# Routing the prompt rows of layer one during sample attention, with the eight sample rows as extra columns of the first two expert tiles

## The reference, cut to what matters

```python
xp = layer_norm(ALPHA * xp + mix_p, ln1_g[i], ln1_b[i])
xs = layer_norm(ALPHA * xs + mix_s, ln1_g[i], ln1_b[i])
xp = layer_norm(ALPHA * xp + moe(xp, ...), ln2_g[i], ln2_b[i])
xs = layer_norm(ALPHA * xs + moe(xs, ...), ln2_g[i], ln2_b[i])

def moe(x, w_router, router_bias, w_gate, w_up, w_down):
    combine = route(t, w_router, router_bias)          # two nonzero weights a row
    h = silu(einsum('td,edf->tef', t, w_gate)) * einsum('td,edf->tef', t, w_up)
    y = einsum('tef,efd->td', h * combine[:, :, None], w_down)
```

## Time and profile before

| what | value |
|---|---|
| median of 3 runs | 1125.22 us (1124.78 to 1127.2) |
| the profiled execution, its own time | 1126.03 us |
| its span, first to last instruction | 1124.4 us |
| mean granted TensorE clock | 0.938 of full |
| PE busy | 978.1 us, 87% of the span |
| DVE busy | 376.1 us, 33% |
| ACT busy | 195.2 us, 17% |
| POOL busy | 94.5 us, 8% |
| HBM traffic | 255.88 MB read, 40.11 MB written |

### The profile page before, as it was taken

One profiled execution on the slowest core, in us unless ns is written; L12 is line 12 of the kernel. 1 busy time (PEld: TensorE's weight loads), 2 busy tenths in 40 slices (PEclk: granted clock), 3 DMA queues, 4 the chain that ended last, 5 costly groups with the idle time before them and its releaser, 6 DMA issues.

```text
span 1124.4 us, 36091 instructions
## 1 busy us (share of the span) xinstructions
PE 978.1 (87%) x15881; PEld 836.7 (74%) x15881; DVE 376.1 (33%) x825; ACT 195.2 (17%) x441; POOL 94.5 (8%) x179
## 2 busy tenths in 40 slices
PE   7979999989998329999999997783399999999975
PEld 6857777754566128999999996562389999999962
DVE  1234443423364612122122122796112122122127
ACT  1233434430052020000000001111200000001010
POOL 0002112141010030000000001200200000000011
PEclk8989999999999559999999999895699999999998
DMA  9513244614311979999999995790599999999935
GB/s 336 189 54 91 89 135 127 206 43 137 92 48 64 412 272 332 361 405 380 403 388 397 381 389 189 269 354 9 194 368 366 407 388 391 393 380 384 396 118 201
DMA packets 80249, 296.26 MB, mean 263 GB/s; under 512 B 10200, under 2 KB 40288, under 8 KB 71871
## 3 DMA queue, kind: packets, MB, share of 16 engines
q1 hardware_dynamic: 52343, 246.53, 58.5%
q10 hardware_dynamic: 19712, 26.75, 7.1%
q0 software_dynamic: 8144, 22.29, 5.7%
HBM read 255.88 MB, written 40.11 MB: 263 GB/s over the span
## 4 chain that ended last, share of the span: by engine, by line
PE 79%; DVE 10%; DMA 4%; issue 3%; POOL 2%; ACT 1%; ACTq 0%; SPq 0%; POOLq 0%; DVEq 0%
PE PS L924 16%; PE PS L945 15%; PE PS L934 15%; PE PS L840 5%; PE PS L598 4%; PE PS L910 3%; PE PS L645 3%; PE PS L661 2%; PE PS L554 2%; PE PS L654 2%; PE PS L576 2%; POOL expert_rows L1106 2%; PE PS L749 1%; PE PS L618 1%; PE PS L635 1%
## 5 line engine op out<-in xcount | busy, mean ns | idle before, releaser
L924 PE MATMUL PS<-arena,ring 128*64 128x96 f32 x4096 | 185.4, 249 | 52.6 <-DVE arena L1759 52.4
L924 PEld LDWEIGHTS PS<-arena,ring 128*64 128x64 f32 x4096 | 175.1, 139 | 59.3 <-issue 59.3
L945 PE MATMUL PS<-arena,ring 128*64 128x96 f32 x4096 | 175.4, 246 | 2.5 <-issue 2.0
L934 PE MATMUL PS<-arena,ring 128*64 128x96 f32 x4096 | 175.0, 246 | 2.8 <-issue 2.8
L945 PEld LDWEIGHTS PS<-arena,ring 128*64 128x64 f32 x4096 | 171.3, 137 | 3.2 <-issue 2.5
L934 PEld LDWEIGHTS PS<-arena,ring 128*64 128x64 f32 x4096 | 171.2, 137 | 3.1 <-issue 3.1
L1759 DVE STREAM_TRANSPOSE arena<-arena 128x768 uint32<-128x768 uint32 x34 | 54.2, 1595 | 166.7 <-ACT arena L1311 138.4
L1784 DVE COPY arena<-PS 128x384 f32<-128x384 f32 x32 | 17.9, 558 | 164.3 <-PE PS L945 164.3
L1313 ACT ACTIVATE arena<-PS 128x384 f32<-128x384 f32 x32 | 15.7, 490 | 265.5 <-PE PS L945 265.5
L840 PE MATMUL PS<-ring,arena 128*128 128x512 f32 x128 | 55.6, 593 | 0.7 <-issue 0.7
L598 PE MATMUL PS<-arena,ring 128*128 128x260 f32 x192 | 46.8, 395 | 2.3 <-POOL ring L1057 2.0
(11 more groups left out here) (276 smaller groups left out, 1030.1 us busy)
## 6 DMA issues: line engine op xcount, KB each, us to landing
ring<-w_gate SPq DMA_DIRECT2D x32, 2048.0 KB, 14.8
ring<-w_up SPq DMA_DIRECT2D x32, 2048.0 KB, 16.1
ring<-w_down SPq DMA_DIRECT2D x32, 2048.0 KB, 17.9
arena<-expert_rows ACTq DMA_DIRECT2D x144, 96.0 KB, 9.0
expert_out<-arena ACTq DMA_DIRECT2D x32, 384.0 KB, 11.8
expert_rows<-ring SPq DMA_DIRECT2D x6, 1920.0 KB, 10.2
ring<-cache_ckv SPq DMA_DIRECT2D x56, 128.0 KB, 2.2
ring<-w_o SPq DMA_DIRECT2D x1, 4096.0 KB, 19.3
```

The costliest lines, as they stand in the source:

```text
L924: last = nc.tensor.matmul(bank(s, KF, CAP)[at:at + 64, f, :], wg[w][:, k, P * f + at:P * f + at + 64], xeT[s][:, k, :], start=(k == 0), st ...
L934: last = nc.tensor.matmul(out[at:at + 64, :], wu[w][:, k, P * f + at:P * f + at + 64], xeT[s][:, k, :], start=(k == 0), stop=(k == KD - 1))
L945: last = nc.tensor.matmul(bank(4 + m // 4, 4, CAP)[at:at + 64, m % 4, :], wd[w][:, f, P * m + at:P * m + at + 64], h[s][:, f, :], start=(f ...
```

## The change

In layer one only, routing is split in two (`choose`, `assign`), each over a range of row tiles:

- The four prompt tiles are routed inside `samples`: `router(0, 3)` moves from u = 3 to u = 1, `choose` over tiles 0 to 3 follows DVE's step u = 1, `counts` moves into PE's step u = 2, and `assign` with the table of tiles follows DVE's step u = 2. POOL scatters the eight prompt row groups as soon as their indices are there.
- The table is made before the sample rows are routed. So `reserve` adds 8 rows to the demand of each expert but the first two, and the sample rows find room if they choose it. `NOV`, the most overflow tiles, goes from 10 to 12.
- The first two experts (tiles 0 and 1) take all eight sample rows as extra columns, 104 instead of 96 (`WIDE`). Their rows come from on-chip transposes of the normalised rows (`turn_sample_rows`), and the results go through `turn_sample_out` and a store of 16 rows of their own.
- The sample rows themselves are routed (`router(0, 4)`, `choose(0, 2, 4, 5)`, `counts(2, ...)`, `assign(0, 2, 4, 5)`) while tiles 0 and 1 run, and scattered to the other experts; a constant `dense_row` points to the 16 rows where they chose expert 0 or 1. Rows of tiles 2 and 3 are loaded after that scatter.
- SP issues the first weights one by one (up and down of expert 0 earlier than before, gate of expert 0 when the pages are done, gate and up of expert 1 after the output projection) and also loads the prompt rows of the first two tiles.
- ACT scales the four prompt row tiles behind sample attention, ahead of the square root of `norm(0, 0, 4)`.
- PE's code has tiles 0 and 1 written out ahead of the loop, which starts at the second pair.
- Scratch regions move in the arena, and `latent_q` uses whole 128-row matmuls in place of halves. Functions without a caller are deleted.

```diff
             def samples():
                 for u in range(BATCHES):
...
-                    if u == BATCHES - 1:
+                    if u == 1:
+                        pe.wait_ge(tp_ev[0], 15)
+                        pe.wait_ge(tp_ev[1], 15)
                         router(0, 3)
+                    elif u == 2:
+                        counts(1, 0, NT - 1)
...
             pe.wait_ge(uv_ev, 1)
             mix(0, 4)
+            turn_sample_rows()
             router(0, 4)
-            counts(0)
             experts(0)
```

```diff
-                with pe.Fori(0, nh) as u:
+                if L == 0:
+                    pe.sem_inc(q["back_ps"], 1)
+                    pe.wait_ge(dense, 2)
+                    tile(0, 0, WIDE)
+                    tile(0, 1, WIDE)
+                    turn_sample_out()
+                with pe.Fori(1 if L == 0 else 0, nh) as u:
...
+            def turn_sample_out():
+
+                pe.wait_ge(S[0]["yT_set"], 2 * DENSE + 2)
+                for m in range(KD):
+                    last = nc.tensor.transpose(bank(1 + 2 * (m // 4), 4, P)[0:DENSE * DB, m % 4, :], yT_s[:, m, :], ident)
+                last.then_inc(dense, 1)
```

DVE:

```diff
                     if u == 0:
                         norm(0, 0, 3, summed=True)
+                    elif u == 1:
+                        v.memset(r_exp[:, E * (NT - 1):], 1.0).then_inc(lg_zero, 1)
+                        choose(0, 1, 0, NT - 1)
+                    elif u == 2:
+                        assign(0, 1, 0, NT - 1)
...
             norm(0, 0, 4)
-            route(0)
...
+            dve.wait_ge(dense, 1)
+            v.tensor_copy(xeT[WIDE][0][:, :, CAP:], bank(1, KD, DB))
+            v.tensor_copy(xeT[WIDE][1][:, :, CAP:], bank(1, KD, DB)).then_inc(dense, 1)
             experts(0)
```

SP, ACT and POOL:

```diff
-                    load_expert(0, 0, 1, gate_free=(pv_ps, BATCHES + 1))
-                    load_expert(0, 1, 0, gate_free=(mix_ps, NT), down_free=(lg_ps, 1))
+                    sp.wait_ge(pv_ps, 3)
+                    sp.dma_start(wu[1], t["w_up"][0, 0].rearrange("(p k) f -> p k f", p=P)).then_inc(q["wu_ld"][1], 16)
+                    sp.wait_ge(pv_ps, 4)
+                    sp.dma_start(wd[1], t["w_down"][0, 0].rearrange("(k p) d -> p k d", p=P)).then_inc(q["wd_ld"][1], 16)
+                    sp.wait_ge(sc_ps, BATCHES)
+                    sp.dma_start(wd[0], t["w_down"][0, 1].rearrange("(k p) d -> p k d", p=P)).then_inc(q["wd_ld"][0], 16)
+                    sp.wait_ge(pv_ps, 5)
+                    sp.dma_start(wg[1], t["w_gate"][0, 0].rearrange("(p k) f -> p k f", p=P)).then_inc(q["wg_ld"][1], 16)
+                    sp.wait_ge(scat, 128)
+                    load_rows(sp, 0, 0, slice(0, CAP))
+                    load_rows(sp, 0, 1, slice(CAP, 2 * CAP))
+                    sp.wait_ge(mix_ps, NT)
+                    sp.dma_start(wg[0], t["w_gate"][0, 1].rearrange("(p k) f -> p k f", p=P)).then_inc(q["wg_ld"][0], 16)
+                    sp.dma_start(wu[0], t["w_up"][0, 1].rearrange("(p k) f -> p k f", p=P)).then_inc(q["wu_ld"][0], 16)
...
                 take_latent_out(BATCHES - 1)
+                act.wait_ge(scat, 128)
+                for i in range(NT - 1):
+                    scale_rows(i)
...
+            hold(pool_e, idx_set, 2)
+            hold(pool_e, zero_st, 16 * (PAIRS - 1))
+            hold(pool_e, ln_out[0], NT - 1)
+            for i in range(NT - 1):
+                scatter(i)
+
             hold(pool_e, uv_ps, 1)
```

More of the change, by code:

```diff
@@ L35 @@
 KOV = (TOK - 1) // CAP
-NOV = 10
+NOV = 12
+DENSE = 2
+WIDE = CAP + DB
 TILES = E + NOV
@@ L720, in latent_q @@
                     for c in range(MKV):
-                        for at in (0, 64):
-                            last = nc.tensor.matmul(bank(7, MKV, PAIRS, 16)[at:at + 64, c, j, :],
-                                                    wukT[:, j, P * c + at:P * c + at + 64], qs[:, j, :], start=True, stop=True)
+                        last = nc.tensor.matmul(bank(7, MKV, PAIRS, 16)[:, c, j, :], wukT[:, j, P * c:P * (c + 1)], qs[:, j, :],
+                                                start=True, stop=True)
                 last.then_inc(ql_ps, 1)
@@ L923, in tile @@
                             for at in (0, 64):
[L924 to L925 removed]
+                                last = nc.tensor.matmul(bank(s, KF, n)[at:at + 64, f, :], wg[w][:, k, P * f + at:P * f + at + 64],
+                                                        x[:, k, :], start=(k == 0), stop=(k == KD - 1))
                     last.then_inc(q["gate_ps"][s], 1)
                     pe.wait_ge(q["wu_ld"][w], 16 * (u + 1))
+                    if n == WIDE and s == 0:
+                        counts(2, NT - 1, NT)
                     for f in range(KF):
[L931 removed]
+                        out = bank(2 + s, KF, n)[:, f, :] if f < KF - 1 else bank(6 + s, n)
                         for k in range(KD):
@@ L1035, in _ @@
                 router(1, i)
-            counts(1)
+            counts(3, 0, NT)
             experts(1)
@@ new lines, in tile @@
+                    if n == WIDE and s == 0:
+                        assign(0, 2, NT - 1, NT)
+                    elif n == WIDE:
+                        next_rows()
+                    dve.wait_ge(q["down_ps"][s], 2 * u + 2)
+                    if n == WIDE:
+                        v.tensor_copy(yT_s[:, 4:8, DB * s:DB * (s + 1)], bank(5, 4, n)[:, :, CAP:])
+                    v.tensor_copy(yT[:, 4:8, :], bank(5, 4, n)[:, :, 0:CAP]).then_inc(q["yT_set"], 1)
+                tile(0, 0, False, CAP if L else WIDE)
@@ L1793, in _ @@
             dve.wait_ge(act_ev, 4 * PAIRS)
-            v.memset(bank(6, NT * E), 0.0).then_inc(lg_zero, 1)
             for i in range(3):
@@ L1820, in _ @@
                     norm(1, 0, step - 4)
-            route(1)
+            choose(1, 3, 0, NT)
+            assign(1, 3, 0, NT)
             dve.wait_ge(mix_ps, 2 * NT)
```

389 lines of the change are left out of this document (222 added, 167 removed).

## The result

| | before | after |
|---|---|---|
| median of 6 runs each | 1125.07 us (1124.15 to 1127.2) | 1136.34 us (1133.42 to 1140.11) |
| ratio | | 1.0099, 95% interval 1.0077 to 1.012 |
| the profiled execution, its span | 1126.03, 1124.4 us | 1138.04, 1136.3 us |
| PE busy | 978.1 us | 994.4 us |

The change costs 11 us; the forecast was a gain of 9. The prediction had the sign wrong. The median lies outside its range, which ended at 1122.5.

A forecast was written before the change was run, and what follows sets the result against it. PE sets the expert phase's pace, after a 35.5 us gap before it that isn't PE's work. Terms -31.5 + 15.0 + 7.5 = -9.0 us give a median of 1116.2, range 1107.5 to 1122.5.

The forecast's parts named there:

- What leaves the gap: Between normalised sample rows and first expert matmul: of 35.5 us, 4.0 remain, so 31.5 us are removed.
- What the sample phase gains: Prompt routing between the steps of sample attention lengthens that phase by 15.0 us, 11.6 of it by the probabilities of u = 3.
- The clock's 3.4 us: After PE idles some 9 us, last weighing, transposes and sample output projections run at half clock: 3.4 us, ends 0 and 5.
- `latent_q` in whole matmuls, costed at nothing: In latent_q, whole matmuls have the same count of columns per weight load, so the edit costs nothing.
- a fall within six idle microseconds: In sample attention before, PE's clock was at half in the six us for which PE had run dry.
- Eight scatters land by 376.3 if nothing slows them: Prompt row scatters of 0.5 MB take 10.2 us on POOL from 362.8 and land by 376.3, costed at nothing.
- The second rival: Scatter shares DMA engines with weights and lands late, at 389; first matmul 2.5 to 6 us later, 1121 us; chance 0.15.
- Its price at the square root, 3.5 us: If the scatter lands late, ACT's scalings hold back the square root for the sample rows by 3.5 us.
- Loaded by 33 (9.0): Rows of tiles 2 and 3, scattered by 24 us into the expert phase, load in 9.0 us, by 33.
- the third rival: Routing the sample rows isn't hidden: half of tile 2 idles if loads take twice 9 us; gain 5, 1120; chance 0.07.
- New code, 3.5 us: First passages through new code, with tiles 0 and 1 written out, cost 3.5 us more, between 0 and 3.7.
- the first rival: No second price of new code and no early fall of the clock: 16 us gained, 1109; chance 0.17.

The follow-up runs named there:

- Experiments 1 and 6: 1: the changed kernel with latent_q in halves again, 1129.71 us, ratio 1.004; 6: the kernel before with latent_q in whole matmuls, 1128.71 us, ratio 1.002.
- experiment 2: The changed kernel with ACT's four scalings of prompt rows moved behind the exponential of the sample rows' router: 1133.59 us, ratio 1.0064.
- Experiment 3: The changed kernel with the sample rows' counts and slots earlier and the rows of tiles 2 and 3 loaded in tile 0: 1126.18 us, ratio 0.9999.
- experiment 5: The kernel before with only PE's first two tiles of layer one written out ahead of the loop: 1132.95 us, ratio 1.0056.
- experiment 4: The changed kernel with latent_q in halves, ACT's scalings later, and rows of tiles 2 and 3 routed and loaded early, all together: 1117.96 us, ratio 0.9918.

## Why the prediction was wrong

Three steps failed: two landing times and one term put at nothing. Point by point:

- **What leaves the gap** held: from the normalised rows (398.42) to the first expert matmul (402.28) 3.9 us, forecast 4.0.
- **What the sample phase gains** held: the probabilities of u = 3 came at 372.3, forecast 369.7, and those of u = 1 had been 2.35 us late already; `choose` ended at 348.8, `assign` ran from 357.8 to 368.1. The clock's 3.4 us held as a sum (2.9), not in its parts: the last weighing took 1.7 us more and the transposes before it 1.0, but the projections behind it only 0.2, as they had been at half clock before too.
- **`latent_q` in whole matmuls, costed at nothing**, failed. It took 5.48 us instead of 2.02, and the clock was at half from 292 to 298. Busy times by stretch of the kernel after:

```profile
288.00:290.00 2.00, 1.26 (x32) 1.02 (x32) 1.97 (x3) 1.08 (x2) 0.00 (x0) 1.00 0.51 160
290.00:292.00 2.00, 2.00 (x26) 1.97 (x24) 1.86 (x5) 0.29 (x1) 0.00 (x0) 0.98 0.03 8
292.00:294.00 2.00, 2.00 (x11) 2.00 (x11) 1.84 (x2) 0.00 (x0) 0.00 (x0) 0.50 0.21 54
```

  Ahead of the fall PE is busy but for one pause of 0.74 us in front of the router, which stands in every kernel here. So it isn't a fall within six idle microseconds, as I had read the earlier trace rows. That reading was wrong for the kernel before as well: in the first of these rows PE is busy for all of 366 to 368 at 0.50, and the clock had fallen in the two microseconds before, of which PE was busy for 1.45:

```profile
364.00:366.00 2.00, 1.45 (x46) 1.34 (x46) 0.44 (x2) 0.40 (x1) 0.31 (x1) 0.71 1.01 426
```

  I reasoned from columns per weight load, and that said nothing about the form's own time at full clock (3.2 us for 2.0). Experiments 1 and 6 show that the edit costs time; how much of the clock's fall is its doing stays open. 5 us in this trace, some 6 by the ratios.
- **"Eight scatters land by 376.3 if nothing slows them"** failed: 391.4. I took the landing of 3.45 us from a stretch in which the scatters had most of the transfer time. DMA queues by stretch (packets, MB, share of the 16 engines), the kernel before while its ten scatters are issued, 393 to 406 us:

```profile
q0 software_dynamic: 1073, 3.94, 75.5%
q1 hardware_dynamic: 348, 1.36, 26.1%
```

  and the kernel after, from the first of its eight to their landing, 364 to 392 us:

```profile
q1 hardware_dynamic: 1128, 6.00, 54.7%
q0 software_dynamic: 1385, 5.12, 45.8%
```

  The DMA engines are full in both; q0 carries POOL's scatters, q1 SP's weights. Beside 6 MB of weights POOL's queue gets 46% of the time in place of 76%, and it has a megabyte of `w_pool` to move besides the 4 MB of rows. The second rival said this, at 0.15, and even its 389 was early. Its price at the square root, 3.5 us, was nearly right: 3.9, and experiment 2 gets it back. What I held against it, that the scatter starts first, went against my own list: two down loads stood there at 359.5 and 359.8, ahead of the scatters at 362.8.
- **"Loaded by 33 (9.0)"** failed: the median of the page stands for a stretch where loads of rows trickle between weights; beside SP's weights (11.17 MB on its queue from 400 to 440 us) and two 0.5 MB loads by POOL the eight loads took 19.8 us. That is "half of tile 2 stands idle when the loads take twice 9 us", the third rival, at 0.07. And the wait fell in a place that none of the steps named: DVE's queue, where the copies of tile 1 stand behind the transpose for tile 2. Experiment 3 gets 11 us back.
- **New code, 3.5 us**: 4.7 in the trace, 6.3 (3.9 to 8.6) in experiment 5 alone, above the end of its bound (3.7). The direction was right, and the first rival, with no such price and no early fall of the clock, is refuted.
- **A missing bound.** The forecast let an earlier first matmul move the end by as much. The median of 14.8 us for a weight load hides a ramp, from 9.9 to 24.8 us in layer one; the slack is used up if the tiles start earlier. In experiment 4 that is 3.1 us of waits.

The three failures sum to 5 + 4 + 11 = 20 us, which is the distance from 1116.2 to 1136.3. Experiment 4, which mends exactly these, has a ratio of 0.9918, or 1115.8 us on the kernel before's 1125.07. The agreement with the forecast is partly luck: new code and the lag of the weights cost some 4 to 6 us that it didn't have, and smaller gains stand against them, such as the first matmul at 395.7 in place of 397.5.

## What to carry over

A landing time is a price only for the traffic it was measured in: before work is moved, read the transfers that will be under way at its new place, and look behind a median of the page for a ramp, by reading the same row in windows. Follow what stands behind every new wait on the same engine's queue: the late rows of one tile stopped the copies of the tile before it. And an edit that is "the same work" for TensorE is costed from its own row or left out: here a change of tile shape cost some 5 of the 20 us.

## What was not expected of the hardware

- The granted clock fell to 0.50 with PE busy for all of the two microseconds before and 1.26 of the two before those, in 32 matmuls of 128 weight rows and 16 columns. These took 0.10 us each at full clock and 0.18 at half, where 64 of half the rows took 0.03 each (2.02 us in all).
- The fall isn't tied to the form alone: of nine profiled executions with halves in the same place it came in four and stayed away in five.
- One written-out pair of tiles costs 6.3 us (3.9 to 8.6) beside a full stream of weights, though it is run once and in a straight line, with three 16 KB packets in each 20 us.
- Scatters of 0.5 MB each had a median of 9.6 us to landing behind 4 MB of down weights and 4.8 us without them; the last one of the kernel after took 18.2 us, against 3.45 before. The share of the engines' time that POOL's queue gets differs with it: 30% and 61%, and 46% against 76%.
- The time from issue to landing of the same 2 MB load grows from 9.9 to 24.8 us between 440 and 680 us, in the sixteen tiles of layer one, with PE hardly waiting; a sixth fewer bytes keep it at 8 to 10.
